# Layer 1's mixer laid out anew: one scaled x, query steps, then key/value steps, with memory and sample attention in beats beside them and column tiles of 32

## The chip, the core and the metric

One core of a Trainium2 chip runs the whole step as one launch. The metric is the device time of that launch in microseconds (us). Every time below comes from one profiled execution of the kernel before, or from the timed runs of it.

## What is computed

One inference step of a two-layer decoder: a prompt of 512 tokens and a sample batch of 8 sequences with 4 new tokens each, 544 columns in all, model width 1024, float32. Layer 0 mixes by a causal convolution and by attention over a memory of 256 rows. Layer 1, where the change lies, mixes by differential attention (6 heads, each with two score maps of width 64 and values of width 128) and again by memory attention (4 heads of width 64). Each layer ends in a gated feed-forward part. Cut to layer 1:

```python
h = _rms(x, norm_mix[1])
k, v = split(_rms(x, norm_kv) @ w_kv, [768])          # k normed per head and half
qf, mq = split(h @ w_in_b, [768])                     # q normed per head and half
p = softmax(where(mask, q·k / 8, -1e30))              # two maps c = 0, 1 of each head
o = (p[:, :, 0] - lam * p[:, :, 1]) @ v
c = _rms(o, subln_g) * (1 - lam_init)
m = softmax(rms(mq)·mem_k[1] / 8) @ mem_v[1]
x = x + concat([c, m]) @ w_out_b
```

The prompt attends to its own keys. A sample sequence attends to 256 past keys and values, two pages of a paged cache found through `page_table`, and to its own 4 new ones; its memory keys and values come from `cache_mem_k` and `cache_mem_v`. The normed keys and the values also go out (`p_k`, `p_v`, `s_k`, `s_v`).

## The kernel before

Activations stand turned: features on partitions, the 544 columns free. A **step** (`mm_step`, L487) makes 128 output features of one projection: weights arrive in `w_raw`, ScalarE (ACT) splits off `w_hi` (L1019), VectorE (DVE) `w_lo` (L1413), and TensorE (PE) runs hi·hi, hi·lo and lo·hi for 8 blocks of 128 input features, in two halves of 272 columns: 48 matmuls into one of two accumulators `acc`. Between the blocks `hooks` insert other PE work. The program is written out by engine, each engine works through its own list in order, and semaphores join them.

Layer 1's mixer is 20 such steps from number `S_B`, ordered key, value, query for each of 6 heads, then two for the memory queries. Keys and values use x scaled by `norm_kv` (`xa_hi`, `xa_lo`, made while layer 0's last part ends); queries use x scaled by `norm_mix` (`xb_hi`, `xb_lo`, L1444), made before DVE takes the first tile (L1490). After a k or q step a tile is squared (ACT L1028), summed over its 64 rows by PE (L499), turned, rooted and turned back (DVE L1430, L1439), scaled (L1592).

Four **beats** fall on a step, one every second block. The function `beat` puts prompt attention there: 24 units, one of 128 query rows of a head. A unit has a score part S (PE L864 into the one score buffer `psX`; DVE mask and maximum L1903 to L1907; ACT exponentials L1316; DVE weights L1675 to L1916), a part T four beats later (PE turns the weights L872, ACT copies L1323) and a part O two beats later again (PE times values L881, DVE copies). A unit starts every third beat.

What does not fit stands behind the 20 steps, one after another:

1. the last units, with the six heads' keys turned to rows for the output (L911);
2. sample attention in 4 groups of 2 sequences: pages turned (PE L937, ACT L1369), scores of all heads with padded queries `qpad` (L966), softmax, fold of the two maps (L973), values (L983); beside it the output norm's sums (L947). The pages come on GpSimd's (POOL) queue (L2136);
3. memory attention, 8 prompt units (scores L696, turn L707, values L716) with the cached sample memory beside them (turn L728, scores L737, values L771), and the output norm's scaling of six heads (L2016, L2018, L2023);
4. eight output steps (`out_part`, L682) and the residual, then the feed-forward part.

Of the kernel before, what the change touches and what calls it, by code (L numbers as in the profile page):

```python
# [28 lines left out]
F32 = mybir.dt.float32  # L29
# [47 lines left out]
S_B = S_FFN[0] + 68  # L77
STEPS = S_FFN[1] + 68
# [4 lines left out]
C_ID, C_BLK, C_MASK, C_NEW, C_FOLD = 0, P, 2 * P, 3 * P, 4 * P  # L83
C_ALL = C_FOLD + 48


def build(nc, a):
    ctx = ExitStack()
    with ctx:
# [34 lines left out]
        gcol, _ = place("gate_tail", [P, 2 * DB + 2, FC])  # L124
        unew, e = place("glu_new", [P, CC, NSA], at=cursor[0] - (4 * (2 * DB + 2) * FC + 31 & ~31))
# [5 lines left out]
        apad, _ = place("fold_padded", [P, 2, PAGES, H, NSA], at=cursor[0])  # L131
# [5 lines left out]
        small, _ = place("small", [P, 3, H * T // 32])  # L137
# [12 lines left out]
        anew, _ = place("fold_new", [NSA, H, NSA], at=e + 4 * 384)  # L150
        exps, _ = place("sample_exps", [P, NKEY], at=e)
        kTb, _ = place("mem_k_cache_t", [P, 2, MC, MEM], at=e)
        prb, e = place("probs", [P, 2, 512], at=e)
        pTt, e = place("probs_t", [P, 4, P], at=e)
        assert e <= endW
# [26 lines left out]
        qT, e = place("diff_q", [P, 2, T], at=regC)  # L182
        mT2, _ = place("mem_mix_b", [P, MC, T], at=regC)
        qnew, e = place("diff_q_new", [P, H, NSA], at=e)
        kT, e = place("diff_k", [P, H, T], at=e)
        od, e = place("diff_o", [P, H, T], at=e)
        orow, _ = place("diff_o_rows", [NSA, CA], at=e)
        vnat, e = place("diff_v", [P, 2, QB, VD], at=e)
        vnew, e = place("diff_v_new", [NSA, H, VD], at=e)
        mq2, e = place("mem_q_b", [P, MC, T], at=e)  # L190
        cs, e = place("fold_scaled", [P, 48], at=e)
# [3 lines left out]
        ctail, _ = place("conv_tail", [NSA, 2, CA], at=e)  # L195
        qpad, e = place("diff_q_padded", [P, 2, 136 * H], at=e)
        mkn, e = place("mem_k_rows", [P, MB, MW], at=e)
        assert e <= regB
        knat, e = place("k_rows_out", [P, QB, CA], at=regA)
        knsam, e = place("k_rows_sample_out", [NSA, CA], at=e)  # L200
        assert e <= regA + 4 * DB * MB * MW
# [7 lines left out]
        for l in range(2):  # L209
# [4 lines left out]
        kpg, e = place("k_pages", [P, 2, PAGES, CA], at=regB)  # L214
        vpg, e = place("v_pages", [P, 2, PAGES, CA], at=e)
        kTs, e = place("k_pages_t", [P, H, NKEY], at=e)
# [24 lines left out]
        xg_hi, xg_lo, xb_h, xb_l = sem("xg_hi"), sem("xg_lo"), sem("xb_h"), sem("xb_l")  # L241
# [14 lines left out]
        at_S, at_nb, at_exp, at_p, at_T, at_aT, at_pv, at_O = (sem("at_" + n) for n in (  # L256
            "scores", "max", "exp", "probs", "turned", "copied", "pv", "out"))
        kp_ld = [sem(f"kp_ld{i}") for i in range(2)]
        vp_ld = [sem(f"vp_ld{i}") for i in range(2)]
        ld_pt = sem("ld_pt")  # L260
        qp_zero, qp_ready, kn_ready = sem("qp_zero"), sem("qp_ready"), sem("kn_ready")
        ds_T, ds_kc, ds_S, ds_nb, ds_exp, ds_p, ds_A, ds_a, ds_pv, ds_row, ds_rc, ds_rT, ds_o = (sem("ds_" + n) for n in (
            "turned", "copied", "scores", "max", "exp", "probs", "folded", "fold_copied", "pv", "rows", "rows_copied",
            "rows_turned", "out"))
        sb_sq, sb_sum, sb_read = sem("sb_squared"), sem("sb_summed"), sem("sb_read")
        kn_T, kn_c = sem("kn_turned"), sem("kn_copied")
# [8 lines left out]
        st_mk, st_mv, st_misc, st_kn, st_ft, st_cs = (sem(n) for n in (  # L275
            "st_mk", "st_mv", "st_misc", "st_kn", "st_ft", "st_cs"))
# [44 lines left out]
        SQ = dict(mem=0, tA=8, ln=14, n1=20, n2=28, tB=36, n3=50)  # L321
# [8 lines left out]
        for s in [S_MEM - 2, S_MEM - 1] + list(range(S_MEM, S_MEM + 8)) + list(range(S_B, S_B + 20)):  # L330
            if s < S_MEM:
                kind = "q"
            elif s < S_MEM + 8:
                kind = "k" if (s - S_MEM) % 4 < 2 else "v"
            else:
                kind = "kvq"[(s - S_B) % 3] if s < S_B + 18 else "q"
            nq = sum(1 for v in tiles.values() if v[0] != "v")
            tiles[s] = (kind, len(tiles), nq if kind != "v" else None)

        def sq_index(s):  # L340
            nq = tiles[s][2]
            return SQ["tA"] + nq if s < S_B else SQ["tB"] + nq - 6

# [28 lines left out]

        block = ctx.enter_context(nc.Block())
# [3 lines left out]

        def beat(b):

            out = []  # L380
            for what, lag in (("S", 18), ("T", 22), ("O", 24)):
                n, r = divmod(b - lag, 3)
                if r == 0 and 0 <= n < H * QB:
                    out.append((what, n))
            return out

        SUB_HEADS = ((0, 1), (2, 3), (4,), (5,))
        KEY_ROWS_BEAT = 84

        def key_rows_sample(i):  # L390
            return acc[1 - i][0:NSA, 1, :]

        LAST_BEAT = 18 + 3 * (H * QB - 1) + 6
# [3 lines left out]
        def _(sp):  # L397
# [21 lines left out]

            win, wmem = a["w_in_a"][0], a["w_mem_kv"]  # L420
# [16 lines left out]
            for l in range(2):  # L437
                wo = a["w_out_a"][0] if l == 0 else a["w_out_b"][0]
                for m in range(KD):
                    load(S_OUT[l] + m, block_cols(wo, m))  # L440
                for g, (g0, n) in enumerate(GROUPS):
# [14 lines left out]
                if l == 0:  # L456
                    for h in range(H):
                        load(S_B + 3 * h, block_cols(a["w_kv"], h))
                        load(S_B + 3 * h + 1, block_cols(a["w_kv"], H + h))
# [1752 lines left out]
```

## Time and profile before

| What | Value |
|---|---|
| Runs, median of 3 (lowest to highest) | 1586.49 us (1583.29 to 1587.37) |
| The profiled execution, its own time | 1585.26 us |
| Its span, first to last instruction | 1583.6 us |
| PE busy | 1465.3 us, 93% |
| DVE busy | 956.6 us, 60% |
| ACT busy | 578.9 us, 37% |
| POOL busy | 122.0 us, 8% |
| Mean granted TensorE clock | 0.957 of full speed |

The span is what the trace shows, the execution's own time holds the 1.7 us around it, and the median of the runs lies 1.2 us above that. A busy PE is one with a matmul in flight; the trace also has the clock that was granted to it, and 1.00 stands for 2.4 GHz. In the chain of work a row gives start, length and what ran; in a timeline a row may merge several instructions of one kind (xN), and the bracket tells how long the engine had been idle and who released it. A float32 matmul stands in the trace as two instructions.

### The profile page before, as it was taken

How to read it: one execution, taken by the hardware profiler on the slowest of the kernel's cores; microseconds unless marked ns; L12 is line 12 of the kernel's file. 1: busy time of each engine (PE TensorE's matmuls, PEld its weight loads, DVE VectorE, ACT ScalarE, POOL GpSimd, SP SyncE). 2: the span in 40 equal slices, each digit the busy share in tenths (PEclk: the TensorE clock that was granted, in tenths of full speed). 3: DMA queues.
4: the chain of work that ended last, by engine and by line, in shares of the span. 5: the costliest groups of instructions: out<-in, count | busy, mean ns of one | idle time of the engine just before them, and what ended most of it. 6: DMA issues, size and time to landing. Idle time of an engine off the chain costs nothing.

```text
span 1583.6 us, 26914 instructions
## 1 busy us (share of the span) xinstructions
PE 1465.3 (93%) x10643; PEld 1383.9 (87%) x10643; DVE 956.6 (60%) x1833; ACT 578.9 (37%) x951; POOL 122.0 (8%) x149
## 2 busy tenths in 40 slices
PE   6899767899999999999999996888999999999997
PEld 5788665799999999999888884666999999999997
DVE  5899888456653664466667774228366635652662
ACT  5544424434331232224445554225243312221232
POOL 3000103120000000001100003201110000000001
PEclk9899888699999999999999998999899999999999
DMA  8111322022233232322322224521132323333222
GB/s 229 49 54 54 93 80 87 12 79 82 85 88 93 82 93 82 92 83 77 91 63 71 70 63 164 180 85 54 41 87 87 93 81 94 87 86 94 81 75 67
DMA packets 209728, 134.85 MB, mean 85 GB/s; under 512 B 5383, under 2 KB 203419, under 8 KB 209583
## 3 DMA queue, kind: packets, MB, share of 16 engines
q1 hardware_dynamic: 201791, 104.94, 23.0%
q0 software_dynamic: 7808, 28.54, 5.6%
q8 instruction: 69, 1.13, 0.3%
q14 instruction: 28, 0.23, 0.0%
q10 hardware_dynamic: 32, 0.01, 0.0%
HBM read 126.25 MB, written 7.85 MB: 85 GB/s over the span
## 4 chain that ended last, share of the span: by engine, by line
PE 72%; DVE 17%; ACT 5%; issue 3%; DMA 1%; POOLq 0%; POOL 0%; ACTq 0%; SPq 0%; DVEq 0%
PE acc L487 55%; PE acc L682 6%; DVE conv_out L1519 4%; DVE w_lo L1413 2%; ACT w_hi L1019 2%; PE acc L983 2%; PE psX L771 1%; DVE softmax_stats L1905 1%; ACT exps L1316 1%; PE psX L966 1%; DVE turned L1430 1%; DVE root_row L1439 1%; PE psT L716 1%; PE psX L639 1%; PE psX L864 1%
## 5 line engine op out<-in xcount | busy, mean ns | idle before, releaser
L487 PE MATMUL acc<-xa_hi,w_hi 128*128 128x272 f32 x1824 | 384.8, 292 | 1.6 <-DVE xa_lo L1444 0.7
L487 PE MATMUL acc<-xa_hi,w_lo 128*128 128x272 f32 x1824 | 378.5, 289 | 0.0
L487 PE MATMUL acc<-xa_lo,w_hi 128*128 128x272 f32 x1824 | 377.6, 289 | 0.0
L1019 ACT ACTIVATE w_hi<-w_raw 128x1024 fp32r<-128x1024 f32 x194 | 205.3, 1058 | 365.0 <-PE acc L487 308.0
L487 PEld LDWEIGHTS acc<-xa_hi,w_hi 128*128 128x128 f32 x1824 | 291.5, 189 | 7.9 <-DVE xa_lo L1444 1.4
L1413 DVE TENSOR_TENSOR w_lo<-w_raw,w_hi 128x1024 fp32r<-128x1024 f32 x194 | 237.7, 1225 | 86.1 <-ACT w_hi L1019 84.6
L487 PEld LDWEIGHTS acc<-xa_lo,w_hi 128*128 128x128 f32 x1824 | 288.0, 189 | 0.0
L487 PEld LDWEIGHTS acc<-xa_hi,w_lo 128*128 128x128 f32 x1824 | 286.2, 190 | 0.0
L487 PE MATMUL acc<-xb_hi,w_hi 128*128 128x272 f32 x832 | 174.7, 291 | 2.0 <-DVE xb_lo L1853 2.0
L487 PE MATMUL acc<-xb_hi,w_lo 128*128 128x272 f32 x832 | 172.2, 288 | 0.0
L487 PE MATMUL acc<-xb_lo,w_hi 128*128 128x272 f32 x832 | 171.6, 288 | 0.0
L1790 DVE TENSOR_TENSOR x_resid<-acc,x_resid 128x544 f32<-128x544 f32 (+1 forms) x64 | 46.4, 725 | 170.8 <-PE acc L487 139.9
L487 PEld LDWEIGHTS acc<-xb_hi,w_hi 128*128 128x128 f32 x832 | 130.6, 188 | 3.1 <-DVE xb_lo L1853 2.4
L487 PEld LDWEIGHTS acc<-xb_lo,w_hi 128*128 128x128 f32 x832 | 130.7, 188 | 0.0
L487 PEld LDWEIGHTS acc<-xb_hi,w_lo 128*128 128x128 f32 x832 | 129.9, 189 | 0.0
L1519 DVE SCALAR_TENSOR_TENSOR conv_out<-glu_ext,params,conv_out 128x512 f32<-128x512 f32 x120 | 86.2, 773 | 0.4
L1247 ACT ACTIVATE gelu<-gate_conv,params 128x544 f32<-128x544 f32 x44 | 33.0, 751 | 133.6 <-DVE gate_conv L1833 133.5
L1833 DVE SCALAR_TENSOR_TENSOR gate_conv<-gate_ext,params,gate_conv 128x512 f32<-128x512 f32 (+1 forms) x176 | 78.8, 498 | 0.1
L1844 DVE TENSOR_TENSOR value<-acc,rstd 128x544 f32<-128x544 f32 x44 | 31.9, 725 | 53.9 <-PE acc L487 53.9
L682 PE MATMUL acc<-xb_hi,w_hi 128*128 128x272 f32 x256 | 57.8, 309 | 6.6 <-DVE xb_lo L1782 4.8
L1251 ACT ACTIVATE xb_hi<-product 128x544 f32 x44 | 29.0, 659 | 89.2 <-DVE product L1850 89.2
L1853 DVE TENSOR_TENSOR xb_lo<-product,xb_hi 128x544 f32 (+1 forms) x44 | 31.9, 725 | 40.5 <-ACT xb_hi L1251 40.5
(332 smaller groups left out, 1968.2 us busy)
## 6 DMA issues: line engine op xcount, KB each, us to landing
w_raw<-in_w_up SPq DMA_DIRECT2D x88, 512.0 KB, 3.8
w_raw<-in_w_down SPq DMA_DIRECT2D x32, 512.0 KB, 3.8
w_raw<-in_w_in_a SPq DMA_DIRECT2D x14, 512.0 KB, 4.8
w_raw<-in_w_down SPq DMA_DIRECT2D x16, 384.0 KB, 3.3
w_raw<-in_w_kv SPq DMA_DIRECT2D x12, 512.0 KB, 3.7
k_pages<-in_cache_k POOLq DMA_DIRECT2D x16, 384.0 KB, 4.5
v_pages<-in_cache_v POOLq DMA_DIRECT2D x16, 384.0 KB, 4.0
w_raw<-in_w_mem_kv SPq DMA_DIRECT2D x8, 512.0 KB, 4.0
```

Source lines behind the costliest of these rows:

```text
L487: last = nc.tensor.matmul(acc[slot][:, c, 0:n], w, x[:, k, c * n:(c + 1) * n], start=(k == 0 and q == 0), stop=(k == kb - 1 and q == 2))
L682: last = nc.tensor.matmul(acc[s % 2][:, c, 0:HT], w, x[:, k, c * HT:(c + 1) * HT], start=(i == 0 and q == 0), stop=(i == KD - 1 and q == 2))
L983: last = nc.tensor.matmul(o_rows(h), apad[:, b2, pg, h, :], vpg[:, b2, pg, h * VD:(h + 1) * VD], start=(g + b2 + pg == 0 and h % 4 == 0), ...
L1019: nc.scalar.activation(whi[:, slot % 2, :], wraw[:, slot, :], ACT.Copy).then_inc(w_hi_ready, 1)
L1247: nc.scalar.activation(gel[:, :], gcv[:, :], ACT.Gelu_apprx_tanh, bias=pcol_at("ffn_conv_b", q)).then_inc(gelu_ready, 1)
L1251: nc.scalar.activation(xb_hi[:, bass.ds(i * 2 + cc, 1), :].rearrange("p o n -> p (o n)"), prod[:, :], ACT.Copy).then_inc(uhi_ready, 1)
L1413: nc.vector.tensor_tensor(wlo[:, slot % 2, :], wraw[:, slot, :], whi[:, slot % 2, :].bitcast(F32), ALU.subtract).then_inc(w_lo_ready, 1)
L1519: ins = nc.vector.scalar_tensor_tensor(out=o, in0=src, scalar=w, in1=o, op0=ALU.mult, op1=ALU.add)
L1790: nc.vector.tensor_tensor(x, acc[b_][:, :, 0:HT], x, ALU.add).then_inc(acc_free, 1)
L1833: ins = nc.vector.scalar_tensor_tensor(out=o, in0=x, scalar=w, in1=o, op0=ALU.mult, op1=ALU.add)
L1844: nc.vector.tensor_tensor(val[:, :].rearrange("p (c n) -> p c n", c=2), acc[(sc + 1) % 2][:, :, 0:HT], rstd[:, :].rearrange("p (c n) -> p ...
L1853: nc.vector.tensor_tensor(lo, prod[:, :], hi.bitcast(F32), ALU.subtract).then_inc(ulo_ready, 1)
```

## The change

The steps of layer 1's mixer stand in another order: the 2 memory query steps, 6 query steps, then key and value of each head in turn (`S_KV` is the first of those 12). There is one scaled x: layer 0's last part scales by `norm_mix` at once, and after the query steps `xa` is scaled over by `norm_kv`, in beats 28 to 31. The mixed result goes to `xa`, and the feed-forward part of layer 1 swaps the roles of `xa` and `xb` (`ffn_tiles`), so that the space of `xb` holds caches, pages and keys.

A table `plan` sets what runs at which beat: memory attention beside the query steps (MS, MT, MO; MK turns cached memory keys; CS, CT, CO are the sample's memory scores, turn and values), prompt units every second beat with T two beats and O three beats after S, the keys' rows (KR, KS), sample attention by pairs of heads over all 8 sequences (KT turned pages, SS scores, ST fold, SO values, SX turned back), the output norm of a head (NQ, NS, NB), the splits of the mixed result (X) and parts of the first two output steps (OP). Within a beat `OUT_PRIORITY` gives the order. All scores share `psX`, all turns one half of `psT`, all outputs the other, each used by one unit at a time.

SS, SO and CS write 32 output rows at a time: four matmuls with 32-column weights into rows 0, 32, 64 and 96, each of another sequence.

```diff
+        for m in range(8):
+            b = 8 + 5 * m // 2
+            at(b, "MS", m), at(b + 2, "MT", m), at(b + 3, "MO", m)
+            at(4 + 2 * m, "MK", m)
+        at(27, "CS", 0), at(29, "CT", 0), at(30, "CO", 0), at(31, "CO", 1)
+        for n in range(H * QB):
+            b = 41 + 2 * n
+            at(b, "S", n), at(b + 2, "T", n), at(b + 3, "O", n)
...
+        SS_AT, KT_AT = (50, 66, 83), (34, 51, 67)
...
-            for what, lag in (("S", 18), ("T", 22), ("O", 24)):
-                n, r = divmod(b - lag, 3)
...
+                    for w in range(4):
+                        s_, j = divmod(w, 2)
+                        for q in range(4):
+                            nc.tensor.matmul(psX[32 * q:32 * q + 32, 0, 0:PAST], qpad[:, q, 24 * w:24 * w + 32],
+                                             kTs[:, j, 4 * s_ + q, :], start=(w == 0), stop=False)
...
-                    for h in range(H):
-                        last = nc.tensor.matmul(psX[:, 0, 0:NKEY], qpad[:, b2, h * P:(h + 1) * P], kTs[:, h, :],
-                                                start=(b2 == 0 and h == 0), stop=(b2 == 1 and h == H - 1))
...
+                        for pg in range(PAGES):
+                            for q in range(4):
+                                nc.tensor.matmul(psT[32 * q:32 * q + 32, 1, j * VD:(j + 1) * VD],
+                                                 afold[:, pg, win + 4 * q:win + 4 * q + 32],
+                                                 pages_[:, q * PAGES + pg, j * VD:(j + 1) * VD],
+                                                 start=(j + pg == 0), stop=False)
...
             for s in range(S_B, S_B + 20):
                 def hooks(k, s=s):
-                    if k % 2 == 0:
-                        for what, n in beat(4 * (s - S_B) + k // 2):
-                            attend(what, n)
-                    if k == 4 and s > S_B:
+                    if k == 2 and s > S_B:
                         tile_hook(s - 1)
...
+                    if k % 2 == 0:
+                        units(4 * (s - S_B) + k // 2)
...
-            for c in range(KD):
-                scaled_hi(xb_hi, c, xT[:, c, :], pcol("norm_mix", 8 + c), xb_h)
...
+                if 28 <= b < 32:
+                    for c in (2 * (b - 28), 2 * (b - 28) + 1):
+                        scaled_lo(xa_lo, xa_hi, c, xT[:, c, :], pcol("norm_kv", c), xg_hi, xg_lo, 24 + c + 1)
...
                 tile_take(s)
                 react(b0)
                 split_lo(s + 2)
                 react(b0 + 1)
-                tile_norm(s)
+                tile_var(s)
                 react(b0 + 2)
+                tile_scale(s)
                 react(b0 + 3)
...
+            pool.wait_ge(mm_done, S_B)
+            pool.memset(qm2[:, :, :, :], 0.0).then_inc(qm_zero, 1)
...
+            for b_ in range(DB):
+                pool.dma_start(*cache_rows_b("cache_mem_k", b_)).then_inc(mc_k, 16)
...
+            def value_pages(n):
+                if n:
+                    pool.wait_ge(out_written, out_no["SO", n - 1] + 1)
+                i, s_ = divmod(n, 2)
+                for x in range(8):
+                    page(vst[:, x, :], "cache_v", 4 * s_ + x // PAGES, x % PAGES, i, vp_ld)
```

Pages now come as the 128 rows of one page and two heads (96 transfers of 128 KB in place of 32 of 384 KB, on POOL's queue as before). The stores of `p_v`, `p_k` and `s_k` move to SyncE's queue, behind the weights' loads, by head or pair.

On VectorE, at the start of layer 1's mixer, stood (`lam` is the attention's weight of the second map, `tile_raw` the first tile taken from the accumulator):

```order
L1439 STREAM_TRANSPOSE rstd<-small 128x544
L1887 TENSOR_TENSOR lam<-lam 128x1
L1889 TENSOR_SCALAR lam<-lam 128x1
L1891 MEMSET lam 128x1
L1893 COPY lam<-lam 64x1
L1444 SCALAR_TENSOR_TENSOR xb_lo<-x_resid,params,xb_hi 128x544 x8
L1490 TENSOR_TENSOR tile_raw<-acc,rstd 128x544
```

and now stands:

```order
L1667 STREAM_TRANSPOSE rstd<-small 128x544
L2149 TENSOR_TENSOR lam<-lam 128x1
L2151 TENSOR_SCALAR lam<-lam 128x1
L2153 TENSOR_SCALAR lam<-consts,lam 128x1
L1739 TENSOR_TENSOR tile_raw<-acc,rstd 128x544
```

The eight passes over x ahead of the first tile are gone from this place.

On TensorE, one group of sample attention behind the steps was (`k_pages_t` are turned pages, `fold_padded` the folded weights):

```order
L966 MATMUL psX<-k_pages_t,diff_q_padded 128x288 x6
L937 MATMUL psT<-consts,k_pages 128x128 x8
L966 MATMUL psX<-k_pages_t,diff_q_padded 128x288 x6
L937 MATMUL psT<-consts,k_pages 128x128 x8
L973 MATMUL psX<-fold_scaled,sample_exps 128x48 x2
L975 MATMUL psX<-fold_scaled,sample_exps 32x48
L937 MATMUL psT<-consts,k_pages 128x128 x4
L983 MATMUL acc<-v_pages,fold_padded 32x128 x24
```

and now, inside a key/value step (L563 is the step's own matmul, L1028 and L1043 a prompt unit's S and O, L1035 its T):

```order
L1043 MATMUL psT<-probs_t,diff_v 128x128 x4
L1052 MATMUL psT<-consts,diff_k 128x128 x4
L1076 MATMUL psX<-k_pages_t,diff_q_windows 32x256 x16
L1080 MATMUL psX<-diff_k,diff_q_windows 32x32 x16
L563 MATMUL acc<-xa_hi,w_hi 128x272 x2
...
L1035 MATMUL psT<-consts,probs 128x128
L1057 MATMUL psT<-consts,diff_k 32x128 x2
L1066 MATMUL psT<-consts,k_pages 128x128 x4
L1028 MATMUL psX<-diff_k,diff_q 128x256 x2
```

The group's scores stand between the blocks of a step, in the beat between two prompt units, and write 32 rows at a time.

## Rows read from the trace of the kernel before

**Rows 1.** The page's slices of the span: PE's busy tenths in 40 slices.

```profile
PE   6899767899999999999999996888999999999997
```

**Rows 2.** Windows of layer 1's mixer: length, busy by engine, clock, DMA.

```profile
780.00:950.00 170.00, 163.47 (x1188) 148.10 (x1186) 123.17 (x267) 86.65 (x175) 5.60 (x8) 0.99 0.24 69
950.00:980.00 30.00, 17.59 (x84) 12.04 (x84) 17.83 (x43) 14.67 (x34) 7.91 (x11) 0.77 0.36 124
980.00:1061.00 81.00, 69.45 (x417) 55.06 (x418) 15.91 (x63) 18.84 (x38) 19.19 (x34) 0.96 0.49 164
...
sum 405.00, PE 360.64 PEld 312.85 DVE 230.52 ACT 172.57 POOL 49.15; mean PE 60.11 PEld 52.14 DVE 38.42 ACT 28.76 POOL 8.19
```

**Rows 3.** The chain of work: start, length, what.

```profile
766.39 0.92 PE psX L508 x4
...
771.28 5.66 DVE xb_lo L1444 x8
...
780.50 7.68 PE acc L487 x48
...
788.72 6.01 PE acc L487 x48
794.73 0.92 PE acc L499 x4
...
836.85 0.70 PE psX L864 x4
...
865.62 0.70 PE psX L864 x4
...
1171.48 0.92 PE psX L508 x4
```

**Rows 4.** PE's groups by line in the mixer: count, busy us, mean ns.

```profile
L966 PE MATMUL psX<-k_pages_t,diff_q_padded 128*128 128x288 f32 x96 | 25.1, 411 | 2.9 <-ACT k_pages_t L1369 2.7
L983 PE MATMUL acc<-v_pages,fold_padded 128*32 128x128 f32 x192 | 24.6, 294 | 0.5 <-DVE fold_new L1998 0.5
...
L737 PE MATMUL acc<-mem_k_cache_t,mem_q_padded 128*128 128x256 f32 x32 | 8.6, 392 | 0.0
```

**Rows 5.** PE's timeline: start, length, form; two score pairs and what follows.

```profile
850.67 1.13 PE L864 MATMUL psX<-diff_k,diff_q 64*128 64x512 f32 x4
851.73 0.71 PE L881 MATMUL psT<-probs_t,diff_v 128*128 128x128 f32 x4
...
1094.72 0.48 PE L696 MATMUL psX<-mem_k,mem_q_b 64*128 64x256 f32 x1
1094.72 0.48 PE L696 MATMUL acc<-mem_k,mem_q_b 64*128 64x256 f32 x1
...
1095.35 0.66 PE L728 MATMUL acc<-consts,mem_cache 128*128 128x128 f32 x4
```

**Rows 6.** One prompt unit after its scores, timelines of DVE and ACT.

```profile
844.70 0.43 DVE L1903 TENSOR_TENSOR psX<-psX,consts 128x256 f32<-128x256 f32 x1 [0.88 <-PE psX L864]
...
846.37 0.58 ACT L1316 ACTIVATE exps<-psX,softmax_stats 128x384 f32<-128x384 f32 x1 [1.85 <-DVE softmax_stats L1907]
...
847.40 0.20 ACT L1316 ACTIVATION_READ_ACCUMULATOR exps<-psX,softmax_stats 128x1 f32 x1
...
849.72 0.16 DVE L1675 RECIPROCAL softmax_stats<-softmax_stats 128x2 f32<-128x2 f32 x1
...
850.44 0.62 DVE L1916 SCALAR_TENSOR_TENSOR probs<-exps,softmax_stats,probs 128x384 f32<-128x384 f32 x1
```

**Rows 7.** PE's timeline where units run with no step beside them.

```profile
953.82 0.70 PE L864 MATMUL psX<-diff_k,diff_q 64*128 64x256 f32 x4 [4.39 <-ACT exps L1316]
...
960.66 0.92 PE L864 MATMUL psX<-diff_k,diff_q 64*128 64x384 f32 x4 [2.25 <-ACT exps L1316]
```

**Rows 8.** POOL's timeline: issues of cache rows and of pages.

```profile
986.34 5.67 POOL L2072 DMA_DIRECT2D mem_cache<-in_cache_mem_k  x8
...
1003.34 0.54 POOL L2136 DMA_DIRECT2D v_pages<-in_cache_v  x1 [10.23 <-issue]
1004.48 0.54 POOL L2136 DMA_DIRECT2D v_pages<-in_cache_v  x1 [0.60 <-issue]
```

More of the change, by code:

```diff
@@ L136, in build @@
         rr, _ = place("root_row", [P, T])
-        small, _ = place("small", [P, 3, H * T // 32])
+        small, _ = place("small", [P, 3, 64])
         rowsum, _ = place("row_sums", [P, 8])
@@ new lines, in build @@
+        for i in range(KD - 2):
+            at(82 + i // 2, "X", i)
+        for i in range(2 * (KD - 2)):
+            at(85 + i // 2, "OP", i)
+        LAST_BEAT = max(plan)
+        def beat(b):
+            return sorted(plan.get(b, ()), key=lambda u: OUT_PRIORITY.index(u[0]))
+        score_no, soft_no, probs_no, turn_no, out_no, square_no = {}, {}, {}, {}, {}, {}
+        for b in range(LAST_BEAT + 1):
+            if b % 4 == 1 and b > 4 and b // 4 <= 20 and tiles[S_B + b // 4 - 1][0] != "v":
+                square_no["tile", S_B + b // 4 - 1] = SQ["tB"] + len(square_no)
+            for u in beat(b):
+                if u[0] in ("MS", "CS", "S", "SS", "NS"):
+                    score_no[u] = len(score_no)
+                if u[0] in ("MS", "CS", "S", "SS"):
+                    soft_no[u] = len(soft_no)
+                if u[0] in ("MT", "CT", "T", "ST"):
+                    probs_no[u] = len(probs_no)
+                if u[0] in ("MT", "CT", "T", "ST", "SX", "KR", "KS"):
+                    turn_no[u] = len(turn_no)
+                if u[0] in ("MO", "CO", "O", "SO", "MK", "KT"):
+                    out_no[u] = len(out_no)
+                if u[0] == "NS":
+                    square_no[u] = SQ["tB"] + len(square_no)
@@ new lines, in output_sum, with units @@
+            def output_sum(h):
+                take_scores(("NS", h))
+                k = square_no["NS", h]
+                pe.wait_ge(sq_ready, k + 1)
+                for c in range(2):
+                    last = nc.tensor.matmul(psX[:, c, 0:HT], ones[:, :], sqt[:, k % 2, c * HT:(c + 1) * HT],
+                                            start=True, stop=True)
+                last.then_inc(sq_used, 1)
+            def units(b):
+                for what, n in beat(b):
+                    if what in ("MK", "MS", "MT", "MO"):
+                        mem_unit(what, n)
+                    elif what in ("CS", "CT", "CO"):
+                        cached_unit(what, n)
+                    elif what in ("S", "T", "O"):
+                        prompt_unit(what, n)
+                    elif what in ("KR", "KS"):
+                        key_rows(what, n)
+                    elif what in ("KT", "SS", "ST", "SO", "SX"):
+                        sample_unit(what, n)
+                    elif what == "NS":
+                        output_sum(n)
+                    elif what == "OP":
+                        out_part(1, n // (KD - 2), [n % (KD - 2)])
@@ L999, in _ @@
[L999 to L1001 removed]
+                units(b_)
             out_section(1)
[L1003 removed]
+            ffn(1, "n3", 4)
         @block.scalar
@@ new lines, in output_unit @@
+            def output_unit(what, h):
+                if what == "NQ":
+                    act.wait_ge(out_taken, out_no["O", QB * h + QB - 1] + 1)
+                    act.wait_ge(turn_copied, turn_no["SX", h // 2 * 2 + 1] + 1)
+                    square(od[:, h, :])
+                elif what == "NS":
+                    root(T, 32)
+                else:
+                    k = (CC, CC + 1, *range(CC))[h]
+                    if h == 0:
+                        act.wait_ge(mm_done, S_B + 20)
+                    if k >= CC:
+                        act.wait_ge(out_taken, out_no["CO", 1] + 1)
+                    else:
+                        act.wait_ge(o_normed, k + 1)
+                    nc.scalar.activation(xa_hi[:, k, :], mT2[:, k - CC, :] if k >= CC else od[:, k, :], ACT.Copy).then_inc(cm_hi, 1)
@@ L2156, in _ @@
+            value_pages(4)
+            for half in range(2):
+                pool.wait_ge(out_written, out_no["KT", 21 + 2 * half] + 1)
+                for x in range(4):
+                    page(kst[:, half, x, :], "cache_v", 4 + 2 * half + x // PAGES, x % PAGES, PAIRS - 1, kp_ld[half])
             add_squares("n3")
```

1061 lines of the change are left out of this document (647 added, 414 removed).

## The prediction, made before the change was run

> **What bounds the kernel now.** I read the slices first: PE is busy nearly throughout, with one long dip, slices 25 to 28 of 40 [rows 1], which is the end of layer 1's mixer. So I cut that mixer out. A sum over squares stands at the same place in the first step of the mixer and in the first step of the feed-forward part behind it, and the two start at 766.39 and 1171.48: the mixer takes 405.1 us [rows 3]. Nothing outside it changes, since swapping two buffers costs nothing where both are free.
>
> The windows of this stretch come next [rows 2]. In the 170 us of the steps PE is busy 163.5, so the steps are bound by PE. Two score parts of the same length, one head apart, start 28.8 us apart [rows 3]; three steps are 3 x 6.01 = 18.0 of it, and 10.7 is one head's hooks and prompt units. Behind the steps it is another picture: between 950 and 980 PE is busy 17.6 of 30 us at clock 0.77, between 980 and 1061 it is busy 69.5 of 81. Over the whole mixer PE is busy 360.6 us and waits 44.4.
>
> Two things can thus shrink: PE's own work, and the waits. DVE (230.5 busy) and ACT (172.6) have room in total, but a stage that is shortened to some 345 us would have DVE at two thirds, so their order matters.
>
> **PE's work, by difference.** The steps, prompt units, turned pages (96 before and after) and memory units are the same count; they move.
>
> - *Sample scores.* Before, 48 matmuls over 288 columns, 25.1 us [rows 4]. After, 48 over 256 columns and 48 over 32, each with 32 weight columns: by columns 22.3 + 2.8 = 25.1 us if one follows another. If four to different rows 0, 32, 64, 96 run together, 6.3.
> - *Sample values.* Before 96 matmuls, 24.6 us [rows 4]. After 96 and 48 more of the same width for the new keys: 36.9 us in a row, 9.2 if four together.
> - *Sample memory scores.* 16 matmuls either way: 8.6 us [rows 4] in a row, 2.15 together.
>
> The trace shows no column tiles at different places, so these are bounds. The nearest row is a pair of matmuls of 64 rows each, on the two halves of the array's rows: both start at 1094.72 and both are over in time for the next at 1095.35 [rows 5]. Such tiles do run together here, in float32. I take "together": saving 18.8 + 15.4 + 6.4 = 40.6 us. One after another it is 25.1 + 36.9 + 8.6 against 58.3 in all, 12.3 more than before.
>
> The Trainium skill, in TensorE: Matmul & The Clock Gate, Part 3 (packing small matmuls), reports 2.38 times for three column tiles, less than three; by that rate (some 3.2 for four) the new work would be 22 in place of 17.7 us, 4 more than my sum. The same skill's TensorEngine Tiling (Array Packing), Key Properties, says that changing the tiling mode drains TensorE; the trace agrees in kind, with the price in the next sentence, and no run here shows the drain of a column tile.
>
> A score pair over 512 columns holds PE from 850.67 to 851.73 [rows 5], 1.06 us, where twice the 0.43 of half that width would be 0.85; I put 0.3 us, an estimate with the entry counted, on each of the 10 new places with column tiles: 3.0. Turning the sample's outputs back by 12 narrow matmuls is new, at most what 2 matmuls onto the values cost, 0.47 for two by the distance to the next row: 2.5.
>
> *Clock.* The tail's gaps cost speed: a clock of 0.77 over 30 us, in which PE is 59% busy, is 46% of the time at the lower level of 1.2 GHz, some 8 busy us done at half speed, so 4 lost; 0.96 over 81 us loses 3 [rows 2]; one early step takes 7.68 in place of 6.01 [rows 3], 1.7. With steps in between I take these 9 us back.
>
> Sum of the work: -40.6 - 9 + 3 + 2.5 = **-44 us**.
>
> **Waits, 44.4 before.**
>
> - *Start.* The first tile waits for eight passes over x, 5.66 us from 771.28 [rows 3], which now lie behind the query steps, where the sample's memory values (beats 30, 31) keep PE at work. What is late next: the first turned memory keys, at beat 4, some 8 us after the mixer's first step, need all 8 cached key loads. POOL issues them after it has zeroed a buffer and 8 issues take 5.67 us [rows 8], then the last must land. I put 3 us of wait there, between 0 (loads early) and 6.
> - *Key/value steps, beats 32 to 79.* A unit now comes every two beats. Its passage outside PE, from mask 844.70 to the maximum's end (the exponentials start 846.37), 1.67, exponentials to 847.60, 1.23, and weights 849.72 to 851.06, 1.34 [rows 6], is 4.3 us with hand-overs; on PE the turn, the turned page and the next scores add some 1.8. So at best 6.1 us from scores to scores. PE's own work per unit there is (39 beats x 1.5 + 5 heads x 9.8 + 34 for the pages, the sample's and the output norm's parts) over 20 units = 7.1. PE still bounds, narrowly. But sample scores and output sums use the same one score buffer, and the values' part stands ahead of a turn in its beat; I price these at 5 us a pair of heads, two pairs: 10.
> - *Tail, from beat 81.* No step covers the last four units. Where units ran alone the scores came 6.84 us apart (953.82 to 960.66 [rows 7]): 27.4, and 4.5 for the third pair's own passage, 0.9 for the last output. Then the last head's copy and square (1.0), sum (0.92), root and row (2.4: from the first sum at the mixer's start to the first pass over x lie 4.9 us [rows 3], less two sums of 0.92 and some 0.6 of small operations), scaling and two splits (0.71 each, as a pass over x [rows 3]: 2.1), and 2.6 behind the head ahead: 42 us. PE's work in it is 25 (12 parts of output steps at 0.75 are 9, units 7, sample 7.4, sums 1.8). So 17 us of wait.
> - *Pages.* 96 issues at 1.14 us apart (1003.34 to 1004.48 [rows 8]) are 109 us of POOL in a stretch of over 200. The value buffer is single: eight issues (9.2 us) and a landing of 4 us must fit in the four beats between two value parts, four beats at 3.5 = 14. I cost it at nothing; its cover is 1 us.
>
> Weights' loads move past the new stores on SyncE's queue; each store waits for something at least a step old, so nothing there.
>
> 3 + 10 + 17 = 30, and 1 for the clock: 31, so **-13.5 us**.
>
> **The sum.** 405.1 - 44 - 13.5 = 347.6 us for the mixer. The profiled execution, 1585.3, becomes 1527.8; the median of the runs stands 1.2 higher, so **1529 us**.
>
> **Rivals.**
>
> *Column tiles do not overlap.* The change then does not do what it says on PE. Work grows by 12.3 in place of -40.6, 53 us more than forecast; but where PE is busy it waits less, so 16 of the 31 go. 37 us worse: **1566**. For it: different sequences mean four different moving operands and four weight loads, and no row shows that. Against it: the row pairs.
>
> *DVE strings a step's tile work into the unit's passage.* DVE works in order: taking a tile, splitting weights, turning and scaling stand between the unit's maximum and its weights; in rows 6 the weights came 2.1 us after the exponentials were read. Such work in a key and a value step is some 6.6 us, estimated from a pass over 544 columns at 0.71 [rows 3]: five of these, two splits of 1024 columns at 1.3 and small ones. If all of it enters, 1.65 a unit, the unit takes 7.8 and PE waits 0.75 x 20 = 15 and 5 in the tail: **1549**. The Trainium skill, TensorEngine Tiling, PSUM Bottleneck, says that tiling speeds TensorE and not the evacuation of its results; that rule is this rival.
>
> *The passage bounds and the clock falls with it: slower.* If sample work on DVE and ACT enters too (1.1 a unit) and the gaps bring PE to 1.2 GHz, as between 950 and 980 [rows 2], PE's 1.8 in the loop becomes 3.6: 6.1 + 1.65 + 1.1 + 1.8 = 10.7 for each of 24 units, 24 x 3.6 = 86 us more: **1615**. It decides from 9.5 us a unit on (57.5 / 24 above 7.1). Against it: between 980 and 1061 PE waited for others at every group and its clock was 0.96.
>
> A better case belongs to the forecast: no waits beside steps and half the tail, some 20 us less, 1509.
>
> **Chances.** Forecast 0.55, tiles in a row 0.17, strung work 0.19, slower 0.07, and 0.02 for mixtures that end within 0.3% (4.8 us, about what a measurement of this kernel can tell from no change). Both middle rivals are still faster: faster 0.91, same 0.02, slower 0.07. The range for 8 in 10 goes from 1503, below the better case, to 1570, above tiles in a row.
>
> **What would show it.** PE busy in the mixer near 317 us; four column matmuls that start within some tens of ns, a pair's sample scores in about 2.5 us (9 says the first rival); scores to scores of prompt units at 7 to 7.5 us between beats 41 and 79 (7.8 the second, over 9.5 the third); the first tile taken within 1 us of the row for x; clock 0.97 or more in the key/value steps; 15 to 20 us of PE's waits after the last step. It is wrong if the mixer is longer than 390 us, or if waits beside the steps exceed 25 us.

## The result, and the profile after

The changed kernel takes 1567.18 us (median of 4 runs, 1566.19 to 1569.24) beside 1584.89 us of the kernel before (4 runs): ratio 0.9888, 95% interval 0.9873 to 0.9903, so 17.7 us faster where 57 were forecast. The profiled span is 1564.5 us (1583.6 before).

Between the two sums over squares that mark layer 1's mixer (764.88 to 1156.06), the windows give length, busy us by engine (and instructions), clock, and the DMA's share and rate:

```profile
764.88:1156.06 391.18, 336.18 (x2615) 293.28 (x2614) 226.65 (x504) 180.90 (x358) 73.21 (x119) 0.91 0.31 90
```

The window begins 0.16 us ahead of the point from which [rows 3] count; measured as there, the mixer fell from 405.1 us to 391.0, not to 347.6. TensorE (PE) is busy 336.2 us (360.6 before, 317 forecast) and not busy for 55.0 (44.4 before, 31 forecast). The clock in it is 0.91. So about 20 us of PE time and 24 us of waits are missing, and both need a cause.

The column tiles are not it. PE's timeline shows a pair's sample scores over 256 columns, 32 instructions on four places of the array; first the first pair's, then the third's:

```profile
919.66 1.93 PE L1076 MATMUL psX<-k_pages_t,diff_q_windows 128*32 128x256 f32 x32
...
1060.35 3.64 PE L1076 MATMUL psX<-k_pages_t,diff_q_windows 128*32 128x256 f32 x32 [3.39 <-ACT exps L1522]
```

The 32 instructions are 16 matmuls (a float32 matmul is two), so four rounds of four tiles, and a round takes 0.48 us, about what one matmul alone took before: 48 over 288 columns in 25.1 us [rows 4] are 0.52 each, by columns 0.46 for 256. The third pair's scores, with PE at its lower level (granted clock 0.50 from 1060.35 to 1064.00), take 3.64 us. The groups by line in the mixer (count | busy us, mean ns) answer to [rows 4]:

```profile
L1076 PE MATMUL psX<-k_pages_t,diff_q_windows 128*32 128x256 f32 x96 | 7.5, 466 | 3.4 <-ACT exps L1522 3.4
L1108 PE MATMUL psT<-v_pages,fold_turned 128*32 128x128 f32 x160 | 5.4, 275 | 3.0 <-issue 3.0
L1115 PE MATMUL psT<-diff_v_new,fold_new 32*32 32x128 f32 x96 | 4.3, 297 | 0.0
L995 PE MATMUL psX<-mem_keys_t,mem_q_windows 128*32 128x256 f32 x32 | 1.9, 382 | 0.0
L1080 PE MATMUL psX<-diff_k,diff_q_windows 128*32 128x32 f32 x96 | 1.6, 213 | 0.0
L1108 PE MATMUL psT<-k_pages,fold_turned 128*32 128x128 f32 x32 | 1.5, 339 | 2.9 <-issue 2.9
```

In sum 22.2 us, where the same work took 58.3 [rows 4]. A mean of 466 ns for an instruction and 7.5 us for 96 of them say that they overlap.

What PE waited for, in the mixer (who waits, for what: us in total, times, longest):

```profile
PE psT L1066 <- DVE diff_o L2230: 7.6, 3, 3.0
PE psX L1132 <- ACT exps L1522: 6.9, 2, 3.4
PE psT L1035 <- DVE probs L2242: 6.4, 3, 3.5
PE psT L1108 <- issue: 5.9, 4, 2.9
PE psX L1132 <- ACT squares L1194: 4.4, 3, 1.9
PE psT L961 <- DMA mem_cache_b<-in_cache_mem_k: 4.3, 1, 4.3
PE acc L761 <- DVE xa_lo L2310: 4.1, 2, 2.6
PE psX L1076 <- ACT exps L1522: 3.4, 1, 3.4
```

No wait is large, and several belong to pieces that need nothing from what they wait for. The first line shows the pattern. L1066 turns a page of keys (KT) into the half of `psT` that all outputs share; it must wait until VectorE (DVE) has copied a prompt unit's output (O, L1043) away. PE's timeline, without the steps' own matmuls:

```profile
888.36 0.38 PE L1043 MATMUL psT<-probs_t,diff_v 128*128 128x128 f32 x2
890.81 0.63 PE L1066 MATMUL psT<-consts,k_pages 128*128 128x128 f32 x4 [2.07 <-DVE diff_o L2230]
...
895.60 0.92 PE L1028 MATMUL psX<-diff_k,diff_q 64*128 64x384 f32 x4
...
901.19 0.63 PE L1066 MATMUL psT<-consts,k_pages 128*128 128x128 f32 x4 [2.53 <-DVE diff_o L2230]
...
904.92 1.31 PE L1028 MATMUL psX<-diff_k,diff_q 64*128 64x512 f32 x4
```

and DVE's at the same place:

```profile
889.32 0.17 DVE L1942 RECIPROCAL softmax_stats<-softmax_stats 128x2 f32<-128x2 f32 x1 [0.46 <-ACT exps L1522]
...
889.98 0.48 DVE L2242 SCALAR_TENSOR_TENSOR probs<-exps,softmax_stats,probs 128x256 f32<-128x256 f32 x1
890.38 0.28 DVE L2230 COPY diff_o<-psT 128x128 f32<-128x128 f32 x1
```

The output was there at 888.74, but DVE's list has the next unit's weights first, which wait for ScalarE's (ACT) exponentials. PE's list is in order, so the step's matmuls behind the page stand too. Scores follow scores at 9.3 to 11.3 us there. The same copy holds the sample's values (L1108), which write to the same half of `psT`: the profile puts their waits down to issue (5.9 us), but each of the four ends 0.1 us after such a copy. The longest one, at 1089.13, stands behind this row of DVE:

```profile
1088.74 0.28 DVE L2230 COPY diff_o<-psT 128x128 f32<-128x128 f32 x1
```

So 13.5 us of waits hang on this one copy. Three more places read alike: a sum over squares (NS, L1132) stands in the same beat behind a unit's scores and so waits for that unit's exponentials in the one score buffer (6.9); the third pair's scores do the same in beat 83 (3.4); the first turned memory keys stand ahead of their loads' landing (4.3).

### The profile page after: what moved, and what is told of

The parts are those of the page before. It is cut to its first block, busy times and chain, and to the rows that moved or that the text cites. A ratio compares the mean times of both kernels' runs of the same rounds, so it can differ in the third digit from the quotient of the medians.

```text
span 1564.5 us, 27782 instructions
## 1 busy us (share of the span) xinstructions
PE 1438.1 (92%) x10845; PEld 1361.5 (87%) x10845; DVE 952.3 (61%) x1821; ACT 586.5 (37%) x960; POOL 148.4 (9%) x206
## 4 chain that ended last, share of the span: by engine, by line
PE 77%; DVE 14%; ACT 4%; issue 3%; DMA 1%; POOL 1%; ACTq 0%; SPq 0%; DVEq 0%
PE acc L563 58%; PE acc L761 6%; DVE conv_out L1768 4%; DVE w_lo L1641 2%; ACT w_hi L1185 1%; PE psX L1028 1%; ACT exps L1522 1%; PE acc L577 1%; DVE softmax_stats L2226 1%; PE psX L848 1%; PE psT L1066 1%; PE psX L717 1%; DVE sample_tap_products L1804 1%; PE psX L1132 1%; PE psT L1043 1%
## 5 line engine op out<-in xcount | busy, mean ns | idle before, releaser
L563 PE MATMUL acc<-xa_hi,w_hi 128*128 128x272 f32 x1600 | 345.7, 298 | 2.1 <-DVE xa_lo L2115 1.0
L563 PE MATMUL acc<-xa_hi,w_lo 128*128 128x272 f32 x1600 | 335.3, 291 | 0.0
L563 PE MATMUL acc<-xa_lo,w_hi 128*128 128x272 f32 x1600 | 334.6, 291 | 0.0
L563 PEld LDWEIGHTS acc<-xa_hi,w_hi 128*128 128x128 f32 x1600 | 257.8, 191 | 19.6 <-issue 10.1
L563 PEld LDWEIGHTS acc<-xa_lo,w_hi 128*128 128x128 f32 x1600 | 255.6, 192 | 0.0
L563 PEld LDWEIGHTS acc<-xa_hi,w_lo 128*128 128x128 f32 x1600 | 254.5, 192 | 0.0
L563 PE MATMUL acc<-xb_hi,w_hi 128*128 128x272 f32 x1056 | 218.7, 288 | 1.0 <-DVE xb_lo L2115 1.0
L563 PE MATMUL acc<-xb_hi,w_lo 128*128 128x272 f32 x1056 | 218.6, 288 | 0.0
L563 PE MATMUL acc<-xb_lo,w_hi 128*128 128x272 f32 x1056 | 217.7, 288 | 0.0
L563 PEld LDWEIGHTS acc<-xb_hi,w_hi 128*128 128x128 f32 x1056 | 166.1, 188 | 1.3 <-DVE xb_lo L2115 1.2
L563 PEld LDWEIGHTS acc<-xb_lo,w_hi 128*128 128x128 f32 x1056 | 165.9, 189 | 0.0
L563 PEld LDWEIGHTS acc<-xb_hi,w_lo 128*128 128x128 f32 x1056 | 164.8, 189 | 0.0
```

The source lines that it names most:

```text
L563: last = nc.tensor.matmul(acc[slot][:, c, 0:n], w, x[:, k, c * n:(c + 1) * n], start=(k == 0 and q == 0), stop=(k == kb - 1 and q == 2))
```

## The experiments

Theory A: pieces that are ready stand behind pieces that are not, at separate places, and the gaps also bring PE to its lower level. Theory B: PE's own work bounds, since column tiles do not overlap. Theory C: one unit's passage through the one score buffer sets the pace, so that a wait taken away comes back as another. All kernels below are the changed kernel with the edit shown. Differences are between medians; the kernel before, timed again beside them, had 1584.9 to 1586.2 us.

**Outputs copied first.**

```diff
 def react(b):
+    for what, n in beat(b):
+        if what == "MO": mem_unit(what, n)
+        elif what == "CO": cached_unit(what, n)
+        elif what == "O": prompt_unit(what, n)
     for what, n in beat(b - 1):
         ...
-        if what in ("MS", "MO"):
+        if what == "MS":
```

(and the same for `CS` and `S`.)

> VectorE copies the outputs of the memory, cached and prompt units ahead of a unit's weights in each beat, in place of behind them. Theory A (a ready piece stands behind one that is not): the four turned pages of the first pair of heads that wait for that copy (7.6 us of TensorE's waits put down to it, at 3.0 us each) no longer wait, the scores around 886 to 916 us come at 7 to 8 us instead of 9.3 to 11.3, and the clock of 0.83 there goes to 0.95 or more: 8 to 12 us less than the changed kernel, about 1557. Theory C (a unit's passage outside TensorE sets the pace anyway): the wait only goes to the turn or the next scores, 0 to 3 us less, and the scores still come 9 us apart. If the copy now holds up the weights, slower by 2 to 5 us.

Measured: 1551.31 us (5 runs; ratio to before 0.9786, 0.9772 to 0.9801), 15.9 us less. The same waits, and the window of the same units (880 to 920 without the edit has 32.41 busy of 40 at clock 0.87):

```profile
PE psT L1066 <- DVE diff_o L2230: 1.8, 3, 0.7
...
PE psT L1108 <- issue: 0.9, 2, 0.4
```

```profile
880.00:914.00 34.00, 31.88 (x286) 27.09 (x285) 22.50 (x62) 19.99 (x46) 6.47 (x12) 1.00 0.36 109
```

The clock is 1.00 there now, and scores follow scores at 6.2 to 7.1 us. The gain is over A's figure: the waits at the value pages (5.9 us put down to issue) fell by 5.0 as well, and the expectation had not tied them to the copy. C falls for this place.

**The third pair's scores in beat 82.** The number in `SS_AT` also places what follows the scores, so the third pair's fold, values, norm and last splits all come one beat earlier.

```diff
-        SS_AT, KT_AT = (50, 66, 83), (34, 51, 67)
+        SS_AT, KT_AT = (50, 66, 82), (34, 51, 67)
```

> The sample's scores of the third pair of heads stand in beat 82, between two prompt units, in place of beat 83, behind the scores of a unit. Theory A: the wait for the one score buffer in front of them (3.4 us) and the gap of 15.3 us between the prompt scores at 1056.26 and 1071.61 shrink to two ordinary gaps of 7 us each with the sample's passage between them; the tail behind the last step falls from 64 us to about 57: 5 to 9 us less than the changed kernel. Theory C (the tail is the sum of the passages of all units through one buffer, in whatever order): 0 to 2 us less. Theory B (TensorE's own work bounds): no change.

Measured: 1555.88 us (ratio 0.9814, 0.9799 to 0.9829), 11.3 us less, above what A expected, and not quite where it expected it. In the changed kernel PE's timeline had, from the last unit's scores on (L1108 with `k_pages` is the second half of the third pair's values, L761 the output part that waits for the last splits):

```profile
1082.69 1.13 PE L1028 MATMUL psX<-diff_k,diff_q 64*128 64x512 f32 x4
...
1089.13 1.48 PE L1108 MATMUL psT<-k_pages,fold_turned 128*32 128x128 f32 x32 [2.93 <-issue]
...
1109.09 0.82 PE L761 MATMUL acc<-xa_hi,w_hi 128*128 128x272 f32 x2 [2.60 <-DVE xa_lo L2310]
```

With the scores in beat 82:

```profile
1070.02 1.94 PE L1108 MATMUL psT<-v_pages,fold_turned 128*32 128x128 f32 x32 [5.11 <-DVE fold_new L2279]
...
1080.71 1.08 PE L1108 MATMUL psT<-k_pages,fold_turned 128*32 128x128 f32 x32
...
1082.77 1.13 PE L1028 MATMUL psX<-diff_k,diff_q 64*128 64x512 f32 x4
...
1098.93 0.81 PE L761 MATMUL acc<-xa_hi,w_hi 128*128 128x272 f32 x2 [2.61 <-DVE xa_lo L2310]
```

The gap of 15.3 us did go, but a new wait of 5.1 us (the values for DVE's copy of the folded weights) took nearly all of it back: the last unit's scores come as late as before (1.8 us earlier, counted from the mixer's start). What is won is that the whole sample passage now lies ahead of them, and from there to the last splits it is 16.2 us in place of 26.4. C, a sum in whatever order, falls.

**The second head's sum of squares a beat later.**

```diff
-                b = SS_AT[i] + late + 2 + (1 if j else 0) + (1 if j and i == PAIRS - 1 else 0)
+                b = SS_AT[i] + late + 2 + (2 if j else 0)
```

> The sum over squares of the second head of a pair comes one beat later, into a beat with no prompt scores ahead of it. Theory A: the two waits of 3.44 us each at 968 and 1035 us go, and with them part of the lower clock of 960 to 980 and 1030 to 1050: 6 to 10 us less. Theory C: the next scores now wait for the sum's reading instead, 0 to 2 us less. Theory B: no change.

Measured: 1560.20 us (ratio 0.9843, 0.9829 to 0.9856), 7.0 us less, in A's range. The line of 6.9 us for the exponentials is gone; the wait of the same sums for ACT's squares grew from 4.4 to 7.4, so about 4 us of waits are won. PE's busy time in the mixer fell from 336.0 to 332.9 us with the same instructions; these 3 us I put down to the clock.

**All column tiles on one place.** What B would have the changed kernel be, made real.

```diff
-  psX[32 * q:32 * q + 32, 0, 0:PAST]      (and three more places)
+  psX[0:32, 0, 0:PAST]
```

> All four column tiles of the sample's scores, values and memory scores write the same 32 rows, one accumulation, so the sample's attention is not the reference's; the count and shapes of the matmuls stay. Theory A and the forecast (tiles at four places run together): the 96 wide score matmuls take 22 us in place of 7.5, the values 37 in place of 9.7, the memory scores 8 in place of 1.9; some 46 to 50 us more of TensorE's work, 35 to 50 us slower than the changed kernel, so slower than the kernel before. Theory B (tiles are serial already): within 5 us of the changed kernel.

Measured: 1608.94 us (ratio 1.0139, 1.0119 to 1.0159), 41.8 us more. The groups:

```profile
L1076 PE MATMUL psX<-k_pages_t,diff_q_windows 128*32 128x256 f32 x96 | 24.0, 413 | 3.4 <-ACT exps L1522 3.4
L1108 PE MATMUL psT<-v_pages,fold_turned 128*32 128x128 f32 x160 | 18.3, 273 | 2.8 <-issue 2.8
L1115 PE MATMUL psT<-diff_v_new,fold_new 32*32 32x128 f32 x96 | 11.6, 269 | 0.0
L995 PE MATMUL psX<-mem_keys_t,mem_q_windows 128*32 128x256 f32 x32 | 7.1, 380 | 0.0
L1108 PE MATMUL psT<-k_pages,fold_turned 128*32 128x128 f32 x32 | 5.3, 346 | 2.9 <-issue 2.9
...
L1080 PE MATMUL psX<-diff_k,diff_q_windows 128*32 128x32 f32 x96 | 3.5, 196 | 0.0
```

69.8 us in place of 22.2, with the mean duration of one instruction nearly unchanged (within 12%): on four places they run side by side, and nearly all of the 47.6 us shows in the time. B is out: without the overlap the new layout would be 24 us slower than the kernel before.

**Turned memory keys two beats later.**

```diff
-            at(4 + 2 * m, "MK", m)
+            at(6 + 2 * m, "MK", m)
```

> Only the eight turns of cached memory keys come two beats later (from beat 6 instead of 4), so the loads of those keys have some 4 us more. Theory A: the wait of 4.3 us for that load at 775 us goes, and with it part of the clock of 0.83 between 770 and 780: 4 to 6 us less than the changed kernel. Theory C (the start only trades one wait for another, as the turns then collide with the first memory units): 0 to 2 us less.

Measured: 1560.36 us (ratio 0.9837, 0.9824 to 0.9850), 6.8 us less. The wait for the load fell from 4.3 to 0.5 us, and the mixer of the profiled execution is 3.5 us shorter (387.5), just under A's 4 to 6 and above C's 0 to 2. The two profiled executions are 5.8 us apart; the other 2.4 lie ahead of the mixer, where nothing was changed and its start varies between 762.1 and 766.8 us over all these profiles. I don't count them for the edit.

**All four edits.**

> Four edits together: outputs copied ahead of weights, the third pair's sample scores in beat 82, the second head's sum of squares a beat later, the turned memory keys two beats later. Alone the first three gave 15.9, 11.3 and 7.0 us less than the changed kernel. Theory A (separate places, each a piece that stands in the wrong order): they add up, 34 to 40 us less, 1527 to 1534, near the forecast's 1529. Theory C (one passage sets the pace, and an edit only removes the same slack again): much less than the sum, 20 us or so, 1547.

Measured: 1530.55 us (1526.61 to 1535.06; ratio 0.9657, 0.9637 to 0.9676), 36.6 us less than the changed kernel, where the four alone sum to 41.0. The mixers of the profiled executions, free of the spread ahead of them, agree: from 391.0 the edits alone take 14.3, 12.2, 7.0 and 3.5 us, 37.0 in sum, and together 36.9, though the profile of all four is the fastest of its five executions (1526.61). The places are separate: A holds and C falls. The mixer:

```profile
762.10:1116.30 354.20, 318.60 (x2615) 277.86 (x2614) 226.29 (x504) 180.76 (x358) 73.08 (x119) 0.96 0.34 99
```

PE runs the same 2615 instructions as before the edits, in 318.6 us instead of 336.2. These 17.6 us go with the clock, 0.96 in place of 0.91, and the waits fell by 19.4, from 55.0 to 35.6. Both parts of the missing time are thus reached by the order of the pieces. The split has a spread: in the three runs that follow, whose mixers hold the same instructions, PE is busy between 317.9 and 326.1 us. Edit by edit, waits and busy time fell by 8.5 and 5.8 us, 6.4 and 5.9, 3.9 and 3.1; the fourth took 4.4 us of wait and no busy time (0.9 more). From the first to the 20th unit's scores PE now has

```profile
872.22:1014.91 142.69, 129.56 (x1169) 108.48 (x1168) 94.50 (x245) 81.25 (x179) 38.43 (x71) 1.00 0.41 121
```

against, in the changed kernel, the same 1169 instructions in

```profile
881.51:1042.20 160.69, 137.78 (x1169) 116.00 (x1168) 95.18 (x246) 81.56 (x179) 38.35 (x71) 0.94 0.37 108
```

a unit every 7.5 us in place of 8.5, at clock 1.00 in place of 0.94.

**Splits and output parts one beat earlier**, on top of the four edits.

```diff
-            at(82 + i // 2, "X", i)
+            at(81 + i // 2, "X", i)
-            at(85 + i // 2, "OP", i)
+            at(84 + i // 2, "OP", i)
```

> The four edits, and the splits of the first six blocks of the mixed result and the parts of the first two output steps one beat earlier (from beats 81 and 84). Theory A: TensorE's idle time in the tail is filled one gap sooner, 1 to 4 us less than the four edits alone. If VectorE's order bounds the tail, the six extra passes (0.71 us each) now stand ahead of a unit's weights and it is 1 to 4 us slower.

Measured: 1531.57 us (1525.34 to 1533.77; ratio 0.9646, 0.9627 to 0.9664). No difference that can be measured. The 1 to 4 us that were expected either way are less than the spread of these runs (8 us), so the run does not decide between the two.

**Splits spread**, on top of the four edits.

```diff
-            at(82 + i // 2, "X", i)
+            at(82 + i // 2 * 2, "X", i)
```

> On top of the four edits, the splits of the first six blocks of the mixed result stand in beats 82, 84 and 86 in place of 82, 83 and 84, so that VectorE reaches the third pair's folded weights earlier. Theory A: the wait of 5.1 us of the sample's values for that copy (at 1040.76 us with all four edits) falls to 2 us or less and part of the clock of 0.52 to 0.66 around it goes: 3 to 6 us less than the four edits alone. If the output parts behind now wait for their blocks, as they stand one beat after them: 0 to 2 us more.

Measured: 1528.84 us (1526.43 to 1533.33; ratio 0.9646, 0.9627 to 0.9665). The wait of 5.1 fell to 3.1, not to 2, and the time is the same as with four edits within the spread, which is too wide (7 us) to show a gain of 2 to 3.

**The sample's memory values two beats apart**, on top of the four edits.

```diff
-        ... at(30, "CO", 0), at(31, "CO", 1)
+        ... at(30, "CO", 0), at(33, "CO", 1)
```

> On top of the four edits, the second half of the sample's memory values (32 matmuls over 16 columns, 3.64 us) stands two beats later (33 in place of 31), so the two halves no longer stand one block apart. If a run of such narrow matmuls brings the clock down with TensorE never idle (matmuls at 0.65 us behind the second half, in place of 0.41, at clock 0.83): the clock between 840 and 860 stays at 0.95 or more, and 1 to 3 us are gained. If the fall has another cause, it stays where it was: no change.

Measured: 1532.28 us (1531.06 to 1533.61; ratio 0.9663, 0.9648 to 0.9677): no gain that the spread would let one see. The clock did not stay up; it fell behind each half (0.91, 0.75 and 0.83 in the three windows of 10 us from 840 to 870). With the four edits it fell behind the second one only, but in other profiles with the halves one block apart it fell behind the first too (last section), so this difference need not be the edit's. (A half is 16 matmuls, 32 instructions, not 32 matmuls.)

## Why the prediction was wrong

**Right.** The column tiles run together, the step that carried 40.6 us: the trace has 36.1 us less there (58.3 to 22.2), and taking the overlap away costs 41.8 us in all. The two matmuls of [rows 5], from which "together" was taken, need 0.63 us where one alone takes some 0.46 by its columns (an estimate from L966 in [rows 4]), so they too overlap less than fully. The serial sum of 70.6 us was right (69.8 in the fourth run). The forecast put the new work at 17.7 us, a quarter of it; four tiles gave a factor of 3.1 in sum (69.8 to 22.2), 3.7 for the memory scores (7.1 to 1.9) and 2.7 for the 32-row tiles of the new values (11.6 to 4.3), so this term was 4.5 us too low. The Trainium skill, TensorE: Matmul & The Clock Gate, Part 3, has 2.38 for three tiles; carried to four, as the prediction's sentence on it did, that gives an estimate of 22 us, and the runs agree with 22.2. The first tile is taken right behind the row for x, as forecast:

```profile
768.53 0.74 DVE L1667 STREAM_TRANSPOSE rstd<-small 128x544 f32<-128x544 f32 x1
...
769.92 0.72 DVE L1739 TENSOR_TENSOR tile_raw<-acc,rstd 128x544 f32<-128x544 f32 x1
```

**Wrong: the waits, forecast to fall from 44.4 to 31.** They rose to 55.0. The tail of the mixer, from the 21st unit's scores to the end of the wait for the last splits, is this window:

```profile
1051.56:1109.09 57.53, 39.42 (x316) 30.36 (x315) 22.54 (x65) 16.32 (x41) 2.16 (x4) 0.74 0.09 24
```

Of the forecast's terms:

- *Key/value steps, 10 us.* This is the largest miss. Between the first and the 20th unit's scores PE is not busy for 22.9 us (160.69 less 137.78). The failing step is "PE still bounds, narrowly": it set a unit's passage (6.1) against PE's work (7.1) as two sums, and left out who stands ahead of whom in a shared buffer. A page that waits for a copy that waits for exponentials is in neither sum and in no price. The output sums on the one score buffer were named and lie within the 10, but not that a sum would stand behind a unit's scores in one beat. With the four edits the figure is 13.1 us and a unit takes 7.5 us, the forecast's 7 to 7.5. So the sums were sound, and the order was not priced.
- *Tail, 42 us with 17 of wait and 25 of work.* From the 21st unit's scores (1051.56) to the end of the wait for the last splits (1109.09) it took 57.5 us. PE is not busy for 18.1 of them, so the wait was forecast nearly right; the work is 39.4 us in place of 25, at clock 0.74 (next paragraph). As for the order, the sum counted the third pair's passage at 4.5 us, beside the units. It stood behind a unit's exponentials, and the next unit's weights stood behind it: scores at 1056.26 and at 1071.61. With the four edits the same stretch is 45.4 us (1024.23 to 1069.66; 33.8 busy, clock 0.80), with the move to beat 82 alone 45.1 (1053.80 to 1098.93).
- *Start, 3 us (0 to 6).* 4.3 were measured: the mechanism was right, the price low by 1.3. Another 4 us of waits beside the query steps had no term.
- *Pages, nothing.* The 5.9 us at the value parts are not waits for a load but for the copy above; with the first edit 0.9 are left.

**Wrong: the clock, 9 us to be won back.** With c the granted clock, the share of a stretch at 1.2 GHz is 2 x (1 - c). Over the mixer that is 2 x 0.09 x 391 = 70 us, where before it was 2 x 0.05 x 405 = 40 (clock 0.95). The failing step is "With steps in between I take these 9 us back": the sum priced the gaps of the old tail and one early step, and put nothing for the new tail's own 17 us of wait, though it had read a clock of 0.77 off the gaps between 950 and 980 [rows 2], nor for gaps beside steps. Measured, the clock is 0.74 in the tail, where PE is 14.4 us longer busy than the 25 forecast, and 0.94 from the first to the 20th unit's scores, where 0.97 or more was expected. With the edits the same instructions take 17.6 us less, which is nearly the whole of the miss in PE's work: 318.6 beside 317 forecast (so near partly by luck, as the column tiles took 4.5 us more than forecast).

**The rivals.** Tiles in a row gives the measured time (1566) by a mechanism that the trace and the fourth run exclude; the sum of waits and lost clock happens to be as large. The stated range, 1503 to 1570, holds 1567 by luck: its upper end was set for that rival. Strung work on DVE was nearer in kind: units came at 8.5 us, slower than its 7.8, and DVE's order was one cause. But it was the place of a 0.28 us copy, not the tile work, which stands where it stood in the run at 7.5 us a unit. The third rival had the lower clock right in kind, but units did not reach its 9.5 us, and with the order changed they take 7.5: the passage does not bound. Both of the prediction's own signs of being wrong showed: a mixer over 390 us (391.0), and waits beside the steps over 25 (35.4 from the mixer's start to the 21st unit's scores).

**Outside the mixer** I expected nothing. From the mixer's end to the span's end it is 412.1 us before and 408.4 after, with PE busy 401.1 in both. The last store's issue ends at 1576.38 of 1583.6 before and at 1560.89 of 1564.5 after, so the difference lies behind it; I did not try what the end waited for. The rest of the 19.1 us between the spans is 14.1 in the mixer and 1.3 ahead of it.

## What to carry to other kernels

Two sums, the work of the busy engine and the passage of one item, do not give the waits of an in-order schedule: go through the list for every shared buffer, and ask of each piece that is ready what stands ahead of it and what that waits for. Where units share a buffer with other pieces, drain the buffer first on the engine that copies, and keep a second user out of the beat in which a unit has just filled it. Price the clock with each gap where PE is nearly always busy: four edits that moved no work gave 36.6 us, about half of it from the clock. Three of them won 0.7 to 0.9 us of PE's busy time with each us of wait; the fourth won the wait alone.

## What the hardware showed beyond the expected

The clock also falls where no wait of PE is noted. Behind the sample's memory values, matmuls over 16 columns (L1014), the step's matmuls run at the lower level. With all four edits the two halves stand one block apart:

```profile
842.74 3.64 PE L1014 MATMUL psT<-probs_t,mem_cache_b 128*128 128x16 f32 x32
...
846.56 0.41 PE L563 MATMUL acc<-xa_lo,w_hi 128*128 128x272 f32 x2
...
847.81 3.64 PE L1014 MATMUL psT<-probs_t,mem_cache_b 128*128 128x16 f32 x32
...
851.63 0.64 PE L563 MATMUL acc<-xa_lo,w_hi 128*128 128x272 f32 x2
...
855.17 0.41 PE L563 MATMUL acc<-xa_hi,w_hi 128*128 128x272 f32 x2
```

Rows of 0.65 us in place of 0.41 last for 3 us, in a window (850 to 860) of 10.00 us busy of 10 at clock 0.83. Here nothing fell behind the first half. In the changed kernel, with the same two halves one block apart, it did:

```profile
850.49 3.64 PE L1014 MATMUL psT<-probs_t,mem_cache_b 128*128 128x16 f32 x32
...
854.44 0.66 PE L563 MATMUL acc<-xa_lo,w_hi 128*128 128x272 f32 x2
```

So it did in the profiles of the first, second, third, fifth and seventh run; in those of the fourth and the eighth it came behind the second half only, as with the four edits. With the halves two beats apart, the last run has it behind each:

```profile
845.47 4.29 PE L1014 MATMUL psT<-probs_t,mem_cache_b 128*128 128x16 f32 x32
...
850.20 0.65 PE L563 MATMUL acc<-xa_lo,w_hi 128*128 128x272 f32 x2
...
858.60 3.81 PE L1014 MATMUL psT<-probs_t,mem_cache_b 128*128 128x16 f32 x32
...
862.85 0.66 PE L563 MATMUL acc<-xa_lo,w_hi 128*128 128x272 f32 x2
```

Ahead of the second one a wait of 0.76 us is noted there, ahead of the first none. So the fall can come behind a single half but need not, and where it comes changes from one profile to the next. That the narrow matmuls are the cause is argued from the place, which moved with them; a run with wider ones in their stead was not made.
